# Stick-breaking suffix sums as two fp32r products instead of one fp32 product

## The reference

```python
def stick_breaking_group(q, k, v):
    # A[t,s] = sigmoid(z_ts) * prod_{s<j<t} (1 - sigmoid(z_tj)), in log space
...
        z = jnp.einsum('bthd,bshd->bhts', qb, kb).astype(jnp.float32) * scale
...
        mask = s_pos[None, :] < t_pos[:, None]
        log_1mb = jnp.where(mask, jax.nn.log_sigmoid(-z), 0.0)
        suffix = lax.cumsum(log_1mb, axis=3, reverse=True) - log_1mb
        A = jnp.where(mask, jnp.exp(jax.nn.log_sigmoid(z) + suffix), 0.0)
        outs.append(jnp.einsum('bhts,bshd->bthd', A, vb))
```

## Time and profile before

| what | us |
|---|---|
| median of 3 runs | 1733.54 (1732.9 to 1734.62) |
| the profiled execution | 1732.56 |
| its span in the profile | 1730.7 |
| mean granted TensorE clock | 0.977 |
| stick-breaking stage, first scores to last output product | 89.8 to 271 |
| suffix sums (L778), 160 records | 8 times about 4.3 |

### The profile page before, as it was taken

The page is one execution under the profiler, slowest core; times in us unless marked ns, Lnnn a source line. Parts: engine busy times, 40 slices in busy tenths (PEclk is TensorE's granted clock), DMA queues, the critical chain, the costliest instruction groups (busy, mean ns, idle before and its releaser), DMA issues.

```text
span 1730.7 us, 26767 instructions
## 1 busy us (share of the span) xinstructions
PE 1643.1 (95%) x9998; PEld 1370.3 (79%) x9998; DVE 1075.6 (62%) x1139; ACT 831.3 (48%) x844; POOL 133.2 (8%) x216
## 2 busy tenths in 40 slices
PE   6999989999975999999999999999999999999995
PEld 5876657987744888888888888888888888888883
DVE  4221554434346677777777777777777777777774
ACT  4243364433321454555545555555555555555553
POOL 0020220000000000100001000010000100000000
PEclk9999989999987999999999999999999999999998
DMA  5111123422066899999999999999999999999993
GB/s 203 49 49 49 49 98 122 143 73 93 25 227 218 278 366 366 377 368 368 370 367 382 364 370 368 368 384 357 373 373 361 387 357 374 369 372 369 369 356 116
DMA packets 134772, 477.05 MB, mean 276 GB/s; under 512 B 10241, under 2 KB 10290, under 8 KB 134706
## 3 DMA queue, kind: packets, MB, share of 16 engines
q1 hardware_dynamic: 123968, 446.72, 69.1%
q0 software_dynamic: 7168, 25.17, 6.1%
q10 hardware_dynamic: 3602, 4.69, 0.9%
HBM read 457.67 MB, written 18.87 MB: 275 GB/s over the span
## 4 chain that ended last, share of the span: by engine, by line
PE 91%; DVE 4%; ACT 3%; issue 1%; DMA 1%; ACTq 0%; POOL 0%; DVEq 0%; POOLq 0%
PE psum L978 23%; PE psum L997 21%; PE psum L1022 21%; PE psum L610 17%; PE psum L789 1%; PE psum L778 1%; PE psum L972 1%; PE psum L964 1%; PE psum L766 1%; PE psum L881 1%; PE psum L901 1%; ACT ring_split L1116 1%; PE psum L915 0%; DVE ring_split L1509 0%; PE psum L889 0%
## 5 line engine op out<-in xcount | busy, mean ns | idle before, releaser
L978 PEld LDWEIGHTS psum<-MIX,ring 128*128 128x128 f32 x4096 | 775.7, 191 | 101.6 <-DVE MIX L1923 1.6
L978 PE MATMUL psum<-MIX,ring 128*128 128x96 f32 x4096 | 726.0, 260 | 1.1 <-DVE MIX L1923 1.1
L997 PE MATMUL psum<-ring_split,xs_hi 128*96 128x512 f32 x512 | 200.3, 437 | 0.0
L1884 DVE TENSOR_TENSOR ring_split<-ring,w_hi_a 128x2048 fp32r<-128x2048 f32 x64 | 146.3, 2288 | 84.2 <-ACT w_hi_a L1366 83.9
L1022 PE MATMUL psum<-ring_split,act_hi 128*96 128x512 f32 x512 | 198.1, 434 | 0.0
L1896 DVE TENSOR_TENSOR ring_split<-ring,w_hi_x 128x2048 fp32r<-128x2048 f32 x62 | 141.9, 2288 | 84.8 <-ACT w_hi_x L1377 84.8
L1884 DVE TENSOR_TENSOR ring_split<-ring,w_hi_x 128x2048 fp32r<-128x2048 f32 x64 | 146.4, 2289 | 72.2 <-ACT w_hi_x L1366 72.2
L610 PE MATMUL psum<-ring_split,H_hi 128*128 128x512 f32 (+1 forms) x512 | 151.2, 379 | 0.6 <-DVE ring L1595 0.6
L1896 DVE TENSOR_TENSOR ring_split<-ring,w_hi_a 128x2048 fp32r<-128x2048 f32 x62 | 141.6, 2284 | 2.5 <-ACT w_hi_a L1377 2.5
L1366 ACT ACTIVATE w_hi_a<-ring 128x2048 fp32r<-128x2048 f32 x62 | 117.7, 1898 | 12.3 <-DMA ring<-in_w_gu 12.3
L1366 ACT ACTIVATE w_hi_x<-ring 128x2048 fp32r<-128x2048 f32 x64 | 121.3, 1897 | 0.0
(11 more groups left out here) (290 smaller groups left out, 2656.8 us busy)
## 6 DMA issues: line engine op xcount, KB each, us to landing
ring<-in_w_gu SPq DMA_DIRECT2D x256, 1024.0 KB, 10.6
ring<-in_w_down SPq DMA_DIRECT2D x128, 1024.0 KB, 12.7
ring<-in_w_in SPq DMA_DIRECT2D x6, 2048.0 KB, 10.2
X<-in_x SPq DMA_DIRECT2D x8, 512.0 KB, 7.6
ring<-in_w_out SPq DMA_DIRECT2D x2, 2048.0 KB, 8.0
ring<-in_w_mk SPq DMA_DIRECT2D x2, 2048.0 KB, 8.9
ring<-in_w_mv SPq DMA_DIRECT2D x2, 2048.0 KB, 7.7
ring<-in_w_mq SPq DMA_DIRECT2D x2, 2048.0 KB, 8.5
```

Of the source, the lines that this page charges most:

```text
L978: return mm(psum[:, dst, q * C:(q + 1) * C], lhsT=gate_w(k // 2)[:, k % 2, f * P:(f + 1) * P], rhs=xsT[:, k, :], start=k == 0 and q == 0, ...
L997: x_last = mm(psum[0:C, L0 + half, :], lhsT=rows_, rhs=cols_, start=k == 0 and n == 0, stop=k == KT - 1 and n == 2, skip_group_check=True)
L1884: v.tensor_tensor(lin_lo(c), lin_w(c), chunk_hi(c).bitcast(F32), ALU.subtract)\
```

## The change

`sb_suffix` now makes its ten products twice in fp32r, once with the high and once with the low part of the masked softplus, both against the minus ones rewritten as fp32r. ScalarE writes the high part into the head's `sb_w` space (free between softplus and exp), VectorE writes the low part in place over `sb_sp`. The matrices of minus ones are rewritten in place by two VectorE copies. On ScalarE the new step of head h+1 stands behind log(h+2) and ahead of `after_log(h)`; on VectorE behind softplus(h+2) and ahead of `after_softplus(h)`. The suffix sums wait for the low part.

```diff
--- before.py
+++ after.py
@@ -193,6 +193,7 @@
         w_glr = sb("w_glr", [P, KT, 16])
         w_glr_hi = sb("w_glr_hi", [P, KT, 16], F32R)
         ident = sb("ident", [P, P])
+        tri_at = nc.sbuf_base
         neg_tri = sb("neg_tri", [P, P])
         neg_ones = sb("neg_ones", [P, P])
         chunk_after = sb("chunk_after", [P, P])
@@ -306,6 +307,11 @@
 
 
         ring_r = nc.alloc_sbuf_tensor_at("ring_split", [P, 6, 4096], F32R, offset=ring_at)
+        scratch_r = ring_r[:, 4:6, :].rearrange("p a b -> p (a b)")
+        sb_hi = [scratch_r[:, 2560 * b:2560 * b + SB_COLS] for b in range(2)]
+        sb_lo = [scratch_r[:, 2560 * b + SB_COLS:2560 * b + 2 * SB_COLS] for b in range(2)]
+        neg_tri_r = nc.alloc_sbuf_tensor_at("neg_tri_r", [P, P], F32R, offset=tri_at)
+        neg_ones_r = nc.alloc_sbuf_tensor_at("neg_ones_r", [P, P], F32R, offset=tri_at + P * 4)
         H_hi = nc.alloc_sbuf_tensor_at("H_hi", [P, KT, T], F32R, offset=h_at)
         H_lo = nc.alloc_sbuf_tensor_at("H_lo", [P, KT, T], F32R, offset=x_at)
         w_glr_lo = nc.alloc_sbuf_tensor_at("w_glr_lo", [P, KT, 16], F32R, offset=glr_at)
@@ -356,6 +362,9 @@
         s_sbln = sem("sb_log_ready")
         s_sbsp = sem("sb_softplus_ready")
         s_sbspm = sem("sb_softplus_masked")
+        s_sbhi = sem("sb_softplus_hi_ready")
+        s_sblo = sem("sb_softplus_lo_ready")
+        s_tri = sem("suffix_masks_placed")
         s_sbsuf = sem("sb_suffix_ready")
         s_sba = sem("sb_weights_ready")
         s_sbam = sem("sb_weights_masked")
@@ -770,14 +779,16 @@
 
             def sb_suffix(h):
 
-                pe.wait_ge(s_sbspm, h + 1)
-                sp_ = sb_sp[h % 2]
-                for i in range(TT):
-                    for i2 in range(i, TT):
-                        o = SB_SEG[i2][2]
-                        last = mm(sb_seg(h, i, i2 - i), lhsT=(neg_tri if i2 == i else neg_ones)[:, :],
-                                  rhs=sp_[:, o:o + T - i2 * P], start=False, stop=True,
-                                  skip_group_check=True)
+                if h == 0:
+                    pe.wait_ge(s_tri, 2)
+                pe.wait_ge(s_sblo, h + 1)
+                for part in (sb_hi[h % 2], sb_lo[h % 2]):
+                    for i in range(TT):
+                        for i2 in range(i, TT):
+                            o = SB_SEG[i2][2]
+                            last = mm(sb_seg(h, i, i2 - i), lhsT=(neg_tri_r if i2 == i else neg_ones_r)[:, :],
+                                      rhs=part[:, o:o + T - i2 * P], start=False, stop=True,
+                                      skip_group_check=True)
                 last.then_inc(s_sbsuf, 1)
 
             def sb_out(h):
@@ -1212,6 +1223,11 @@
                 ch.link(go(w, w, ACT.Exp, scale=-1.0))
                 go(w, w, ACT.Ln, bias=one_col[:, :]).then_inc(s_sbln, 1)
 
+            def sb_split_hi(h):
+
+                act.wait_ge(s_sbspm, h + 1)
+                go(sb_hi[h % 2], sb_sp[h % 2], ACT.Copy).then_inc(s_sbhi, 1)
+
             def sb_exp(h):
                 act.wait_ge(s_sbsuf, h + 1)
                 act.wait_ge(s_sbsp, h + 1)
@@ -1246,6 +1262,7 @@
 
             sb_log(0)
             sb_log(1)
+            sb_split_hi(0)
             for h in range(SB_HEADS):
                 for g in FILL[2 * h]:
                     fill(g)
@@ -1254,6 +1271,8 @@
                     fill(g)
                 if h + 2 < SB_HEADS:
                     sb_log(h + 2)
+                if h + 1 < SB_HEADS:
+                    sb_split_hi(h + 1)
                 after_log(h)
             mix_hi(7)
 
@@ -1655,8 +1674,18 @@
                     mix_lo(6)
                     split_lo("out1", 1)
 
+            def sb_split_lo(h):
+
+                dve.wait_ge(s_sbhi, h + 1)
+                v.tensor_tensor(sb_lo[h % 2], sb_sp[h % 2], sb_hi[h % 2].bitcast(F32), ALU.subtract)\
+                    .then_inc(s_sblo, 1)
+
+            dve.wait_ge(s_const, 1)
+            v.tensor_copy(neg_tri_r[:, :], neg_tri[:, :]).then_inc(s_tri, 1)
+            v.tensor_copy(neg_ones_r[:, :], neg_ones[:, :]).then_inc(s_tri, 1)
             sb_softplus(0)
             sb_softplus(1)
+            sb_split_lo(0)
             for h in range(SB_HEADS):
                 for part in range(2):
                     for g in FILL[2 * h + part]:
@@ -1666,6 +1695,8 @@
                 took(("av", h), v.tensor_copy(MIX[r:r + 64, 4 + h // 2, :], bank(("av", h))[r:r + 64, :]))
                 if h + 2 < SB_HEADS:
                     sb_softplus(h + 2)
+                if h + 1 < SB_HEADS:
+                    sb_split_lo(h + 1)
                 after_softplus(h)
 
             mix_lo(7)
```

## The result

The changed kernel takes 1745.25 us in the median of 6 runs (1740.17 to 1747.7) and the kernel before 1733.73 (1732.9 to 1734.62): a ratio of 1.0058, 95% interval 1.0047 to 1.0069. It is slower, as forecast, but by 11.5 us where 4.8 were forecast, and it lies outside the range.

A forecast was written before the change was run, and what follows sets the result against it. TensorE was taken to bound the kernel, with the stick-breaking heads' chain of waits deciding. Waits less savings, 9.6 - 4s = +2.6 us, plus 2.2 for the clock, on 1733.5 gave 1738.3 us, range 1732.5 to 1743.4.

The forecast's parts named there:

- Where the suffix sums count: Stick-breaking heads: sums on the chain in heads 0, 2, 3, 5, 7, each 4.3 to 4.5 us; not in 1, 4, 6.
- The price of the fp32r sums: TensorE, per head: two fp32r sets take 2.51 us in place of fp32's 4.26.
- s: Time saved per head by fp32r suffix sums where TensorE decides: 1.75 us.
- The term for the 128-column product: Short fp32r products in the suffix sums: 0.08 us each, from transposes 0.082 apart; bounds 0.067 and 0.213.
- The rival of short products at fp32's price: Suffix sums: 128-column fp32r products gain nothing over fp32, 0.213 us each; +7.5 us, 1741.0, 1743.2 with the clock; chance 0.20.
- The added work and the new wait: Per head a 1.2 us ScalarE copy and 1.49 us VectorE subtract; sums wait for the low part, queued behind next softplus.
- Head by head: Heads 0 to 7: +2.15, +1.2, -1.75, -0.15, +1.2, -0.55, +1.2, -0.7 us; sum +2.6.
- The clock: Head 0: the 3.9 us stop makes the clock fall once more, +2.2 us, bounds 0 and 2.5.
- The range: Whole kernel: 1732.5 to 1743.4 us, from vanished spell below to slow short products with the clock above.
- slow short products: Suffix sums: short fp32r products at fp32's rate, +7.5 us; chance 0.20.
- the fall at head 0: Clock drops to 1.2 GHz after head 0's 3.9 us stop, +2.2 us; rival of no fall, 1736.1, chance 0.24.
- the slow spells of heads 4 and 6: Half-clock stretches there; rival: they move with the waits and one shrinks or vanishes, -2.4 us; chance 0.10.

The follow-up runs named there:

- products_only_busy: products_only with products by a zero matrix added in heads 1, 4 and 6, where its TensorE stood: 1722.14 us, ratio 0.9929.
- before_busy: The kernel before with products by a zero matrix added in heads 4 and 6, where TensorE stood: 1730.07 us, ratio 0.997.
- split_fp32: The changed kernel with its copy, subtract and wait, but the suffix sums as one fp32 product, low part zero and unused: 1745.46 us, ratio 1.0061.
- products_only: The changed kernel's two fp32r sets without copy, subtract and wait, the softplus written as fp32r and read by both sets: 1729.19 us, ratio 0.9966.
- early_split_2_busy: Changed kernel, copy before next logarithm, subtract before next softplus (behind output copy except head 6), fill before first sums, zero products in heads 1, 4, 6: 1722.91 us.
- after_busy_more: The changed kernel with products by a zero matrix where TensorE stood, extended where an earlier such run still had the clock down: 1734.33 us.
- early_split: The changed kernel with the copy of head h+1 ahead of log(h+2), the subtract ahead of the copy of out(h) and softplus(h+2): 1738.05 us, ratio 1.0014.

## Why the prediction was off, point by point

- **Where the suffix sums count.** Right. On the chain in heads 0, 2, 3, 5 and 7, hidden in 1, 4 and 6; products_only_busy against before_busy gives 7.9 us for five heads, and nothing in the other three.
- **The price of the fp32r sums.** In the chain head 2's sums take 2.72 us where fp32 took 4.33, so s is 1.6; forecast were 2.51 for 4.26, 1.75. The term for the 128-column product was mis-sized. The first set of head 2 in order of time, with its starts in the first column (a merged row shows the shape of its first product; x3 is 384, 256 and 128 columns):

```profile
159.37 0.39 PE L789 MATMUL psum<-ring_split,neg_tri_r 128*128 128x512 f32 x1
159.59 0.51 PE L789 MATMUL psum<-ring_split,neg_ones_r 128*128 128x384 f32 x3
159.94 0.40 PE L789 MATMUL psum<-ring_split,neg_tri_r 128*128 128x384 f32 x1
160.18 0.34 PE L789 MATMUL psum<-ring_split,neg_ones_r 128*128 128x256 f32 x2
160.35 0.33 PE L789 MATMUL psum<-ring_split,neg_tri_r 128*128 128x256 f32 x1
160.52 0.22 PE L789 MATMUL psum<-ring_split,neg_ones_r 128*128 128x128 f32 x1
160.58 0.56 PE L789 MATMUL psum<-ring_split,neg_tri_r 128*128 128x128 f32 x2
```

  The short product itself is left after 0.06 us (160.52 to 160.58), but the one behind it holds the array longer: 384 columns take 0.24 (159.94 to 160.18) instead of 0.173, 256 columns 0.17 (160.35 to 160.52) instead of 0.120. A short product thus costs about 0.06 + 0.055, some 0.11, not 0.08. The weight loads around the short products start 0.11 apart in the same trace (159.89 and 159.99, 160.64 and 160.75), as those of L719 do in the kernel before. The Trainium skill ("TensorE: Matmul & The Clock Gate", LDWEIGHTS) has a load take its columns over 1.2 GHz, which is 107 ns for 128 columns; this trace agrees. That it is the weight load which holds up the next product is my reading; no run here shows it apart. The transposes of the earlier trace rows, from which I took 0.08, were the wrong neighbour, and L719 the right one. With s at 1.6 instead of 1.75 the sum is 0.6 higher. The rival of short products at fp32's price is out.
- **The added work and the new wait.** Right. The copy took 1256 ns and the subtract 1480 (1.2 and 1.49), and the waits for the low part were 3.8, 1.1, 1.4 and 0.5 us before heads 0, 1, 3 and 7 and none before 2 and 5 (forecast 3.9, 1.3, 1.6, 0.9, none). The wait of head 6, 4.6 us, costs nothing, as the chain has ScalarE there.
- **Head by head.** The sum of waits and products is +3.3 with the clock out of the way, forecast +2.6 (3.2 with the measured s); no head is off by more than 0.3. So that the kernel got slower is right for the stated reason.
- **The clock.** Here the prediction failed. It let the clock fall once more, at head 0, for 2.2 us. After minus before, less the same with zeros, is 1.6 in head 0, 1.5 in head 1, 2.6 in head 5 and 1.7 in head 7, together 7.4; the medians say much the same, 11.5 apart without zeros and 4.3 to 4.9 with them. In head 0 it was nearly right, and split_fp32 has that fall too, for 1.7. The step that failed is that I looked for a fall only at the one long new stop.
  - The step began with a wrong reading of the kernel before. I said that the clock fell after two stops of 1.9 and 2.1 us. But the earlier trace rows is a piece from the middle of that stretch; it begins at 208.98, and the second stop ran from 208.79 to 210.88, so it had only begun. One stop of 1.9 us with small work behind it was enough in the kernel before, so the shorter stops had to be looked at too.
  - The other falls that cost time follow such shorter stops, in heads 1, 4 and 7; the long one behind head 4 runs on through head 5, where its cost shows. Head 1 shows best what the faster sums have to do with it. Both the changed kernel and split_fp32 wait 1.1 us ahead of the sums. The sums of 2.7 to 3.0 us are then over so early that TensorE stands another 1.96 us, until 133.66, and the clock falls at 135.19; behind fp32 sums of 4.6 us it stands 0.33, and the clock stays up.
  - The length of a stop alone doesn't decide. In head 7 the kernel before stands 1.98 us ahead of its output product and keeps its clock, while the changed kernel, with stops of 0.5, 0.5 and 1.1 us behind its short sums, loses it.
  - So the fault was to price the faster product only as time saved. What comes with it, more standing and lighter work in front of it, was put at nothing.
- **The range** had its upper end from slow short products with the fall at head 0, and let the slow spells of heads 4 and 6 only shrink, by 2.4; nothing in it stood for further falls. The changed kernel also spreads more (1740.17 to 1747.7) than the kernel before (1732.9 to 1734.62), and this goes with the clock: the mean granted clock of its span was 0.967 in its slowest execution and 0.972 in its fastest, and 0.977 in the profiled one of the kernel before. Where the falls lie I know for one execution of each kernel only.

What stays open: how much of the extra clock loss comes from TensorE standing longer, and how much from fp32r products being a lighter load than the two-record fp32 products for the same time. products_only loses 7 us to the clock (1729.19 against 1722.14) with no wait added, the kernel before 4.8, so the faster sums alone bring 2. The changed kernel loses 11 (1745.25 against 1734.33), so with these sums the waits bring 4 more. With fp32 sums they bring nothing in the sum: split_fp32 loses about 4 (1745.46 against 1730.07 and 11.3 of waits). No run held the standing time equal and changed the type alone.

## What to carry to other kernels

A new wait on an engine's queue costs by its place: the same copy and subtract cost 11 us behind the next head's logarithm (split_fp32) and under 1 us ahead of it, where ScalarE and VectorE stood waiting for TensorE, once a fill was moved ahead of the first sums (early_split_2_busy against products_only_busy). Before pricing a faster TensorE step, mark where TensorE will stand after it and what light work is around that place, for the clock can take the gain back. A short stop can count: here the clock fell behind single stops of 1.3 to 2.2 us, though not behind every one. In a stage that stops and starts, products by zero in the stops are a cheap test of how much of the time is the clock's, and here also a gain of 4.8 us by themselves.

## What the runs showed of the hardware that I had not expected

- The clock went to 1.2 GHz at 157.7 and 181.6 us of products_only with TensorE never standing in the microseconds ahead: behind 2.7 us of fp32r sums and 2 us of a product with 17 rows (L715), and behind such sums, 2 us of L722 with 256 moving columns and 2 us of L728 with two. Four more such starts stand at the same two places, at 161 in after_busy_more, 164 and 188 in early_split and 179 in early_split_2_busy. The kernel before has the same small products behind 4.3 us of fp32 sums and keeps its 2.4 GHz there. That is six starts in the profiles of ten kernels with fp32r sums and none in the four with fp32 sums, one execution of each: a hint at the sums, and no proof.
- Products by a matrix of zeros hold the clock: the granted clock of the stage went from 0.95 to 1.00 with 12 of them. After fp32r sums one stretch of 3.4 us at half clock can be left even so (after_busy_more, early_split_2_busy).
- A 128-column fp32r product costs about 0.11 us, half of it in the product behind it.
